# A two-layer gated DeltaNet and Mamba-2 trunk in fp32: a new order of ScalarE's weight roundings in the SSD loop, and a split scaling in the gate stages

## What is computed

```
def ple_add(h, p_i, w_proj, w_gate, norm_w):
    e = rmsnorm(p_i @ w_proj, norm_w)
    gate = jax.nn.sigmoid((h @ w_gate).astype(jnp.float32))
    return h + (e * gate).astype(h.dtype)

def ssd_mixer(hn, conv_buf, S0, w_in, conv_w, conv_b, ..., w_out, chunked):
    proj = hn @ w_in
    z, xbc, dt_raw = proj[..., :o1], proj[..., o1:o2], proj[..., o2:]
    xbc, new_buf = causal_conv(xbc, conv_buf, conv_w)
    xbc = jax.nn.silu(xbc + conv_b).astype(f32)
    ...                                  # dt = softplus, A = -exp(A_log)
    y, S = mix(xs, dt, A, Bm, Cm, S0)    # chunked for the prompt, per token for the samples
    y = y + D_skip * xs
    y = y.reshape(Bsz, L, SSD_D_INNER) * jax.nn.silu(z.astype(f32))
    ...                                  # rmsnorm by group
    out = y.astype(hn.dtype) @ w_out

def trunk(...):
    for i in range(DEPTH):
        hn = rmsnorm(h, norm_w[i]).astype(h.dtype)
        h = h + mixer_i(hn)
        h = ple_add(h, p[i], ple_w_proj[i], ple_w_gate[i], ple_norm_w[i])
    y = rmsnorm(h, final_norm_w)
```

## Time and profile before

| what | value |
|---|---|
| median of 3 runs | 2509.16 us (2508.77 to 2509.59) |
| the profiled execution: its time | 2507.85 us |
| its span, first to last instruction | 2506.0 us |
| busy: PE, PEld, DVE, ACT, POOL | 95%, 89%, 59%, 51%, 70% |
| mean granted TensorE clock | 0.974 of full speed |
| HBM traffic over the span | 164 GB/s |

### The profile page before, as it was taken

How to read it: one execution, slowest core, us unless ns; L and a number is a source line. 1 busy time by engine, 2 the same in 40 slices (tenths; PEclk the granted TensorE clock), 3 DMA queues, 4 the chain that set the end, 5 groups by cost and what they waited for, 6 DMA issues and landing times.

```text
span 2506.0 us, 58534 instructions
## 1 busy us (share of the span) xinstructions
PE 2377.4 (95%) x21280; PEld 2218.6 (89%) x21280; DVE 1483.8 (59%) x2961; ACT 1268.6 (51%) x2209; POOL 1764.5 (70%) x2236
## 2 busy tenths in 40 slices
PE   5899999999999999999999899999999999899997
PEld 4899999999999999989989898898889888899897
DVE  7566666666666666630336476787778779513354
ACT  4555555555555555543344455554555556333443
POOL 5455666665555666559889777787778778598895
PEclk9899999999999999999999999999999999899998
DMA  5444444444444444445444365466556555454433
GB/s 199 142 152 152 152 152 149 148 150 151 152 151 152 152 146 150 138 150 176 153 155 142 134 225 175 164 234 217 170 174 235 198 159 208 144 195 158 156 134 113
DMA packets 126771, 410.83 MB, mean 164 GB/s; under 512 B 21344, under 2 KB 37984, under 8 KB 122112
## 3 DMA queue, kind: packets, MB, share of 16 engines
q1 hardware_dynamic: 80784, 294.49, 34.2%
q10 hardware_dynamic: 45936, 115.64, 13.6%
HBM read 363.47 MB, written 46.61 MB: 164 GB/s over the span
## 4 chain that ended last, share of the span: by engine, by line
POOL 50%; issue 31%; PE 15%; DVE 3%; ACT 1%; POOLq 1%; ACTq 0%; DVEq 0%
POOL wl L325 50%; PE psj L348 5%; PE psj L350 4%; PE psj L349 4%; DVE xl L1350 1%; DVE Y L1732 1%; POOLq L329 0%; ACT wh L779 0%; DVE h L1947 0%; DVE h L1893 0%; POOLq L323 0%; PE psA L675 0%; PE psA L726 0%; PE psj L638 0%; ACT xh L798 0%
## 5 line engine op out<-in xcount | busy, mean ns | idle before, releaser
L325 POOL TENSOR_TENSOR wl<-ring,wh 128x256 fp32r<-128x256 f32 x2232 | 1764.3, 826 | 716.2 <-ACT wh L779 713.2
L348 PE MATMUL psj<-xh,wh 128*128 128x288 f32 x4400 | 1364.0, 310 | 77.0 <-POOL wl L325 33.7
L349 PE MATMUL psj<-xl,wh 128*128 128x288 f32 x4400 | 1309.9, 298 | 0.0
L350 PE MATMUL psj<-xh,wl 128*128 128x288 f32 x4400 | 1305.4, 297 | 0.0
L348 PEld LDWEIGHTS psj<-xh,wh 128*128 128x128 f32 x4400 | 836.0, 190 | 135.2 <-issue 57.7
L779 ACT ACTIVATE wh<-ring 128x1024 fp32r<-128x1024 f32 x558 | 578.3, 1058 | 543.0 <-PE psj L350 516.7
L349 PEld LDWEIGHTS psj<-xl,wh 128*128 128x128 f32 x4400 | 839.2, 191 | 1.9
L350 PEld LDWEIGHTS psj<-xh,wl 128*128 128x128 f32 x4400 | 840.1, 191 | 0.0
L860 ACT ACTIVATE arena<-psj 128x256 f32<-128x256 f32 x112 | 42.7, 381 | 195.6 <-PE psj L350 168.3
L1774 DVE SCALAR_TENSOR_TENSOR arena<-arena 128x256 f32<-128x256 f32 x144 | 123.5, 897 | 2.6
L1707 DVE TENSOR_TENSOR h<-h,psj 128x288 f32 x32 | 14.6, 455 | 154.4 <-PE psj L350 154.4
(11 more groups left out here) (339 smaller groups left out, 2867.6 us busy)
## 6 DMA issues: line engine op xcount, KB each, us to landing
ring<-weights_d SPq DMA_DIRECT2D x558, 512.0 KB, 3.3
h<-gstate_d ACTq DMA_DIRECT2D x16, 1024.0 KB, 6.2
gst_s_d<-h ACTq DMA_DIRECT2D x16, 1024.0 KB, 3.9
h<-sstate_d ACTq DMA_DIRECT2D x32, 512.0 KB, 5.3
sst_s_d<-h ACTq DMA_DIRECT2D x32, 512.0 KB, 5.3
arena<-g_rows_d ACTq DMA_DIRECT2D x16, 864.0 KB, 5.9
arena<-s_rows_d ACTq DMA_DIRECT2D x8, 1152.0 KB, 9.8
h_spill_d<-h ACTq DMA_DIRECT2D x2, 2304.0 KB, 8.0
```

Of the source, the lines that this page charges most:

```text
L325: ins = pool.tensor_tensor(wl[:, s, n:n + 2], ring[:, s, n:n + 2], wh[:, s, n:n + 2].bitcast(F32), ALU.subtract)
L348: pe.matmul(out, w_h, xh[:, kt, :], start=(kt == 0), stop=False)
L349: pe.matmul(out, w_h, xl[:, kt, :], start=False, stop=False)
L350: mm = pe.matmul(out, w_l, xh[:, kt, :], start=False, stop=(kt == KT - 1))
```

## The change

In `ssd_body` the rounding of tile k+2 is split. Its first half is rounded at the start of `took(k)`, before the wait for the whole of tile k, and its second half at the end. For k = 2 the first half (half 8 of the round) is rounded still earlier, right behind the copy of B. The rest of `took(2)` moves ahead of the Silu of the sample columns, and `took(3)` ahead of the copies `s_s1` and `sRO`. In the gate stages VectorE scales two PLE tiles, makes the first two gated tiles, and then scales the other 14.

```
@@ ssd_body (ScalarE)
+                def first_half(k):
+                    upper(mt, 2 * per, 2 * (t0 + k + 2))
+
+                def took(k, between=None, first=True):
+
+                    if first:
+                        first_half(k)
                     tile_wait(mt, per, t0 + k)
...
                     if between is not None:
                         between()
-                    ahead(mt, per, t0 + k + 2)
+                    upper(mt, 2 * per, 2 * (t0 + k + 2) + 1)
...
                 act.activation(sa["BT"], psA[:, 0:2 * P], ACT.Copy).then_inc(S("s_btc"), 1)
+                first_half(2)
                 act.wait_ge(S("s_r_in"), m * 16 + 16)
...
                 decays(0)
                 act.wait_ge(S("s_sconv"), m + 1)
+                took(2, first=False)
                 act.activation(sCV[:, :, SEQ:T], sCV[:, :, SEQ:T], ACT.Silu).then_inc(S("s_scv"), 1)
                 if full:
                     act.wait_ge(S("s_cv"), m + 1)
                     s_load_pack(m + 1)
-                took(2)
-                if not full:
-                    took(3)
+                took(3)
                 act.wait_ge(S("s_s"), m * 2 + 1)
                 act.activation(sS1, psA[:, :], ACT.Copy).then_inc(S("s_s1"), 1)
                 act.wait_ge(S("s_ro"), m + 1)
                 act.activation(sRO, psE[:, :], ACT.Copy).then_inc(S("s_roc"), 1)
-                if full:
-                    took(3)
@@ ple (VectorE)
-                for i in range(KT):
-                    ins = dve.scalar_tensor_tensor(eb[:, i, :], eb[:, i, :], prm[:, wc + i:wc + i + 1], dRE,
-                                                   ALU.mult, ALU.mult)
-                do.link(ins)
+                def scaled(a, b):
+                    for i in range(a, b):
+                        ins = dve.scalar_tensor_tensor(eb[:, i, :], eb[:, i, :], prm[:, wc + i:wc + i + 1], dRE,
+                                                       ALU.mult, ALU.mult)
+                    do.link(ins)
...
+                scaled(0, 2)
                 gated(0, 0)
                 gated(0, 1)
+                scaled(2, KT)
```

More of the change, by code:

```diff
@@ L1225, in ssd_body @@
                 u_of = {2: 0, 3: 1, 4: 2, 5: 3, 8: 4, 9: 5} if full else {}
-                def took(k, between=None):
+                def first_half(k):
[3 more added lines that the diff above has]
+                        first_half(k)
                     tile_wait(mt, per, t0 + k)
```

## The result

| | before | after |
|---|---|---|
| median of the runs timed together | 2508.97 us (2503.77 to 2509.85) | 2486.82 us (2479.92 to 2494.14, 6 runs) |
| ratio, 95% interval | | 0.9915 [0.9902, 0.9928] |
| profiled execution, its time | 2507.85 us | 2482.71 us |
| its span | 2506.0 us | 2480.9 us |
| mean granted clock | 0.974 | 0.983 |

The change is faster by 22 us, in sign as forecast and in size less than half of the 51 us. It lies outside the range of 2450 to 2472 us. Each engine does what it did (ScalarE has seven more table loads, 2216 instructions instead of 2209), and the clock has gained, as the page of after says (compare).

A forecast was written before the change was run, and what follows sets the result against it. TensorE, busy 95%, was taken to lose time to idling and half clock, through order, not load. SSD loop 39.7, short round 0 and gate stages 11.4 us sum to 51.1, giving 2458 us, range 2450 to 2472.

The forecast's parts named there:

- Half 8 ready in time: Step 32 of each round: half 8 ready at 1602.5, TensorE asks at 1603.84, so the whole 3.83 us stall goes.
- `s_pr` "at about 1606.2": VectorE's signal behind the Silu comes after TensorE asks at 1605.7: a new wait, taken as 0.6 us a round.
- The half clock is gone too: Behind step 32's stall: the new wait is too short to lower the clock, so 2.6 us a round are won.
- `s_s1` and half 9 hidden: Later in the round: copy `s_s1` starts near 1607.3, needed near 1609; half 9 through at 1606.5, needed past 1612.
- The new table load costs nothing: Top of each round: load, rounding, load end at 1582.7, inside ScalarE's wait for tile 0 until 1583.15; cost nothing.
- The other first halves, "worth nothing by itself": Other tiles' earlier roundings fill GpSimd's pauses where TensorE does not wait: no gain, but GpSimd keeps a larger lead.
- The short round at 0, -2 to +3: Short last round: VectorE's 14.00 us piece still delays `decayed(1)`; gain taken as 0, bounds -2 (later) and +3 (earlier).
- The gate stages, 11.4 us: Both gate stages: the 3.26 and 3.84 us stalls go with the half clock behind them, gaining 4.9 and 6.5 us.
- (b): Rival: a new wait (`s_pr`, `s_s1` or GpSimd) replaces part of the old, 9 to 16 us less gain; chance 0.11.
- (a): Rival: the half clock has another reason and stays, only idle time is won, 29.7 us, 2479 us; chance 0.07.
- (c): Rival: slower, late transfers of first halves hold up ScalarE's takes and TensorE stops for a bank, 2514 us; chance 0.02.
- (d): Rival: another input of step 32 is as late as half 8, so 2505 to 2509 us; chance 0.02.

The follow-up runs named there:

- e9: The kernel before with the new gate stages and one loop edit, half 8 rounded ahead of ScalarE's wait for `s_tok`: 2442.29 us, ratio 0.9738.
- e3: The change with a 1024-column dummy copy in place of half 9's rounding, which comes behind the Silu in full rounds: 2458.25 us, ratio 0.9808.
- e6: The change with half 8 rounded ahead of the wait for `s_tok` and half 9 behind the Silu: 2451.42 us, ratio 0.9771.
- e2: The kernel before with only the gate part of the change, the SSD loop as before: 2497.4 us, ratio 0.9965.
- e4: The change with half 9 rounded behind the Silu, without a stand-in copy: 2452.6 us, ratio 0.9783.
- e7: e3 with a further table switch and a copy of 480 columns on ScalarE ahead of the Silu: 2477.44 us, ratio 0.9883.
- e8: e6 with VectorE, in the short round, making 4 rests of Y ahead of `decayed(1)` and 12 behind it: 2447.39 us, ratio 0.9753.
- e1: The SSD part of the change alone, gate stages as in the kernel before: 2493.8 us, ratio 0.9951.
- e5: The change with half 8 rounded one step earlier, ahead of ScalarE's wait for `s_tok`: 2482.39 us, ratio 0.9893.
- e10: The change itself run once more, with no edit: 2480.79 us, ratio 0.9895.

## Why the prediction was wrong, point by point

- **What bounds the kernel**: right. The stall was a matter of order; e9 takes it away by moving one rounding, with the half clock, and comes out 66 us under the kernel before.
- **Half 8 ready in time**: right. Line 325 is waited for 1.7 us in all.
- **ScalarE's Silu 2.3 us later**: right, 2.26.
- **`s_pr` "at about 1606.2", a new wait of 0.5 to 0.6 us, bounds 0 and 1.5**: this is the step that failed. It added the 2.3 us to VectorE's end in the earlier trace rows and kept VectorE's durations. Those rows had been recorded in the very pause of GpSimd, 4.74 us, that the change fills with half 9. A slowdown of these products by GpSimd was put at nothing, without a reason, though the same prediction reckons with one in the short round ("runs faster if GpSimd is done sooner"). The term measures 2.63 to 3.39 us, 0.65 of it ScalarE's (as worked out) and 2.0 to 2.7 VectorE's slower work: the products took 3.1 to 3.9 us instead of 1.12. A warning was to be had from the same trace: two products of 128 x 256 take 0.75 us in the pause of GpSimd, 0.38 each, and one of 128 x 288 takes 0.86 us in the gate stage, where GpSimd works without a pause (16 pieces in one row of 14.47 us from 1330.73).
- **The half clock is gone too**: followed from 0.6 us, and fell with it. With the real wait it stayed behind 5 of 7, some 6 us over the six rounds. With the wait at 0.64 (e3) the clock did what the step says, and a round was 79.6 us for a forecast of 79.3. The stretch ahead of the first line 372 and the six rounds of e3 gained 5.2 and 33.8 us on the kernel before, 39.0 for a forecast of 39.7: the rest of the loop's sum stands.
- **`s_s1` and half 9 hidden**: right, no wait at line 699 and none over 0.6 us for GpSimd.
- **The new table load costs nothing**: right. ScalarE's timeline at the top of the round:

```profile
1575.59 1.28 ACT L779 ACT_TABLE_LOAD   x1 [0.53 <-DMA ring<-weights_d]
1576.88 1.06 ACT L779 ACTIVATE wh<-ring 128x1024 fp32r<-128x1024 f32 x1
1577.97 1.28 ACT L1239 ACT_TABLE_LOAD   x1
1580.04 0.41 ACT L1239 ACTIVATE arena<-psj 128x288 f32<-128x288 f32 x1 [0.79 <-PE psj L350]
```

ScalarE still sat idle for 0.79 us ahead of the take, the operation behind a load begins 0.01 us after it, and the second load 0.03 us after the rounding ahead of it. In e3, with the same loads, a round is 79.6 us for a forecast of 79.3. The 1.38 us for a drain, from the Trainium skill's "ScalarE: Activation LUTs", What ACT_TABLE_LOAD costs, do not show here, and the 16 us that they would have cost did not come.

- **The other first halves, "worth nothing by itself"**: right in the rounds. That they cost nothing does not hold with the moved takes beside them: e9, without either, is 9 us faster than e6.
- **The short round at 0, -2 to +3**: from the seventh line 372 to the second gate stage it gave 2.1 us, inside, but by luck. The wait for VectorE's rests at its first output tile was not seen, it grew to 7.53 us, and up to the eighth line 372 3.8 us were lost. Behind it 5.9 us were won, 2.5 of them because the wait for `decayed(1)` fell from 2.9 to 0.4 us, where the prediction had named one longer than 2.92 us as a sign of being right.
- **The gate stages, 11.4 us**: 9.0 in the profiled execution, 10.1 in e2's, where the whole difference of the medians is 9.7. Both stalls went. What was short in the first stage is the clock: the low stretch at its start is 6.8 us long where it was 3.4. In the second, TensorE waits 3.6 us less, for 3.84 forecast, and is busy for 1.9 us less, for 2.6; why the half clock gave less back there was not looked into.
- **The rivals**: (b) had the right place, `s_pr`, at half its size; it was priced at 9 to 16 us, and the loop fell short by some 24. (a), (c) and (d) did not come: without a long stop the clock stays at full in the loop (e3, e9).

## What to carry to other kernels

A duration read from a trace belongs to what the other engines did at that time. When a change fills a pause of GpSimd, look at which VectorE operations with two operands in SBUF stood in that pause, and price them as in a stretch where both work; if a signal for TensorE hangs on them, put the GpSimd work behind it. And move as little as the finding asks for: the one half that was late, moved alone beside the same gate stages, gave three times the gain of the whole reordering (66 against 22 us).

## What the runs showed of the hardware

Small products of VectorE suffer more from GpSimd than their own length would suggest. The six ahead of `s_pr` (128 x 32, 24, 16 and 8, then two of 128 x 256) take 1.12 us together in every full round in which GpSimd is idle or sets in during their last 0.2 us (before, e2, e3, e4, e6, e7, e8, e9), and 3.0 to 3.9 us in every full round in which it works beside them (the change, e1, e5, e10). GpSimd and VectorE in the change, one instruction to a row:

```profile
1602.26 0.72 POOL L325 TENSOR_TENSOR wl<-ring,wh 128x256 fp32r<-128x256 f32 x1
1602.27 0.75 DVE L1841 TENSOR_TENSOR arena<-arena 128x24 f32<-128x24 f32 x1
...
1603.02 0.73 POOL L325 TENSOR_TENSOR wl<-ring,wh 128x256 fp32r<-128x256 f32 x1
1603.03 0.75 DVE L1841 TENSOR_TENSOR arena<-arena 128x8 f32<-128x8 f32 x1
```

Before, each of the four took 0.16 to 0.19 us. These two set in 0.01 us behind a piece of GpSimd and ended 0.03 to 0.04 us behind its end; the one between them (128 x 16) set in 0.07 us ahead of the next piece and took 0.16 us. The piece that set in together with the fifth of the six products took 0.99 us instead of 0.73, and that product its usual 0.41, so GpSimd can be the one that waits. A product with one of its two operands in PSUM (line 1834 of the change, 128 x 256) took 0.42 us beside GpSimd and 0.42 without it. The Trainium skill has this in "SBUF — State Buffer", section SBUF: two separate sides: the port pair that the two engines share is an exclusive lock that one of them has for a whole instruction, and a VectorE instruction with two SBUF inputs asks for it. The rows agree; how the loss depends on the length of GpSimd's piece was not tried.

TensorE's granted clock, by what stood ahead at step 32: behind stops of 3.83 us it fell 14 times of 14 (before, e2), behind stops of 2.3 to 4.1 us 23 times of 35 (the change, e1, e5, e7, e10), behind 0.64 us never. In this middle range it falls in one round and not in the next: it fell behind a stop of 2.31 us (e5) and not behind one of 3.50 (e10). In one execution it falls more often than in another, 5 of 7 and 3 of 7 with the same kernel. The kernels with such stops spread over 6 to 14 us, those with waits of 0.64 us or none over 2 to 5 (e3, e4, e6, e8, e9), and the kernel before, where every stop has its half clock, over 2 to 7.
